# Strassen-like gate and up products: partial sums kept in one PSUM bank, with two alternating bank sets

## The reference, cut to what matters

```python
def channel_and_ple(h, p, g_ffn, w_gate, w_up, w_down, g_ple, w_ple_gate, w_ple_proj):
    n = rms_norm(h, g_ffn)
    h = h + (jax.nn.silu(n @ w_gate) * (n @ w_up)) @ w_down
    gate = jax.nn.sigmoid(rms_norm(h, g_ple) @ w_ple_gate)
    return h + gate * (p @ w_ple_proj)
```

## Time and profile before

| | |
|---|---|
| median of three runs | 2497.94 us (2497.43 to 2499.43) |
| span of the profiled execution | 2496.2 us |
| PE busy | 2467.4 us, 99% of the span, 20366 matmuls |
| DVE busy | 1755.7 us, 70% |
| ACT busy | 942.3 us, 38% |
| POOL busy | 255.1 us, 10% |
| granted clock of TensorE, mean | 0.996 of full speed |

### The profile page before, as it was taken

How to read it: one execution, slowest core, us unless ns; L and a number is a source line. 1 busy time by engine, 2 the same in 40 slices (tenths; PEclk the granted TensorE clock), 3 DMA queues, 4 the chain that set the end, 5 groups by cost and what they waited for, 6 DMA issues and landing times.

```text
span 2496.2 us, 51722 instructions
## 1 busy us (share of the span) xinstructions
PE 2467.4 (99%) x20366; PEld 2452.8 (98%) x20366; DVE 1755.7 (70%) x2206; ACT 942.3 (38%) x1226; POOL 255.1 (10%) x281
## 2 busy tenths in 40 slices
PE   7999999999999999999999999999999999999998
PEld 7999999999999999999999999999999999999998
DVE  5777787778787899888888888888433323456433
ACT  5344334333433454444444444444322221233331
POOL 1120111011110000000000000000000000143000
PEclk9999999999999999999999999999999999999999
DMA  6352333233343424333333334343665443233331
GB/s 210 120 159 93 129 109 127 98 121 110 119 149 99 150 93 162 122 132 135 118 135 118 135 120 146 122 150 110 223 220 165 161 146 117 80 90 108 108 114 68
DMA packets 99886, 324.02 MB, mean 130 GB/s; under 512 B 18274, under 2 KB 18786, under 8 KB 99312
## 3 DMA queue, kind: packets, MB, share of 16 engines
q1 hardware_dynamic: 72288, 250.25, 30.4%
q0 software_dynamic: 26672, 70.69, 8.1%
q10 hardware_dynamic: 864, 2.24, 0.2%
HBM read 286.80 MB, written 40.65 MB: 131 GB/s over the span
## 4 chain that ended last, share of the span: by engine, by line
PE 82%; DVE 9%; issue 3%; DMA 3%; ACT 1%; DVEq 0%; SPq 0%; ACTq 0%
PE acc L570 15%; PE acc L574 14%; PE acc L572 14%; PE acc L774 12%; PE acc L775 12%; PE acc L773 12%; DVE tmp L1525 2%; DVE wlo L1293 1%; DMA wraw<-in_w_down 1%; DMA skew<-skew_dram 1%; DVE tmp L1298 1%; ACT whi L929 1%; DVE q_both L1410 1%; DMA hid<-in_x_tiles 1%; PE aux L619 1%
## 5 line engine op out<-in xcount | busy, mean ns | idle before, releaser
L1293 DVE TENSOR_TENSOR wlo<-wraw,whi 128x1024 fp32r<-128x1024 f32 (+1 forms) x276 | 333.5, 1209 | 361.3 <-ACT whi L929 360.8
L929 ACT ACTIVATE whi<-wraw 128x1024 fp32r<-128x1024 f32 (+1 forms) x276 | 285.2, 1034 | 667.6 <-PE acc L574 593.1
L773 PE MATMUL acc<-xb_hi,whi 128*128 128x260 f32 x1228 | 347.9, 283 | 2.3 <-DVE xb_lo_t L1692 2.3
L774 PE MATMUL acc<-xa_lo,whi 128*128 128x260 f32 x1228 | 348.7, 284 | 0.0
L775 PE MATMUL acc<-xa_hi,wlo 128*128 128x260 f32 x1228 | 348.7, 284 | 0.0
L773 PE MATMUL acc<-xa_hi,whi 128*128 128x260 f32 x1228 | 347.3, 283 | 0.6 <-DVE wlo L1643 0.6
L775 PE MATMUL acc<-xb_hi,wlo 128*128 128x260 f32 x1228 | 347.5, 283 | 0.0
L570 PE MATMUL acc<-slots_a,whi 128*128 128x260 f32 x1536 | 312.8, 285 | 0.3 <-DVE wlo L1293 0.3
L574 PE MATMUL acc<-slots_a,wlo 128*128 128x260 f32 x1536 | 308.9, 282 | 0.0
L572 PE MATMUL acc<-slots_a,whi 128*128 128x260 f32 x1536 | 308.9, 283 | 0.0
L1104 ACT ACTIVATE whi<-wraw 128x1024 fp32r<-128x1024 f32 x176 | 186.4, 1059 | 223.0 <-PE acc L775 120.7
(11 more groups left out here) (309 smaller groups left out, 5111.4 us busy)
## 6 DMA issues: line engine op xcount, KB each, us to landing
wraw<-in_w_in SPq DMA_DIRECT2D x96, 512.0 KB, 3.6
blocks<-in_w_gate SPq DMA_DIRECT2D x88, 512.0 KB, 5.9
blocks<-in_w_up SPq DMA_DIRECT2D x88, 512.0 KB, 5.3
wraw<-in_w_down SPq DMA_DIRECT2D x48, 448.0 KB, 3.4
wraw<-in_w_out SPq DMA_DIRECT2D x32, 512.0 KB, 3.6
wraw<-in_w_ple_gate SPq DMA_DIRECT2D x32, 512.0 KB, 3.5
slots_b<-f_dram SPq DMA_DIRECT2D x28, 520.0 KB, 4.5
f_dram<-sig_t POOLq DMA_DIRECT2D x22, 520.0 KB, 3.2
```

What stands on the lines that cost most here:

```text
L773: mm(to, w_h, hi, start=p == 0, stop=False)
L774: mm(to, w_h, lo, start=False, stop=False)
L929: on(whi[:, u % HILO, 0:width], wraw[:, u % RAW, 0:width], ACT.Copy).then_inc(s_whi, 1)
L1293: V.tensor_tensor(wlo[:, u % HILO, 0:width], wraw[:, u % RAW, 0:width], whi[:, u % HILO, 0:width].bitcast(F32), ALU.subtract).then_inc(s_w ...
```

## The change

The operands' signs are turned so that products that are only added can be summed by PE in one bank. A pair's units write to three banks instead of four: units 0, 2, 4 and 6 to one bank (`z`), without starting it anew after unit 0; units 3 and 5 to a second (`x`); unit 1 to a third (`w`). Between them the partial sums are copied out: after unit 0 (`q0`), after unit 2 (`v2`), after unit 3 (`p5`) and after unit 6, all by ACT; DVE makes three combinations, after units 1, 4 and 5. PE waits for each copy before it adds to the bank again: unit 2 for `q0`, unit 4 for `v2`, unit 5 for `p5`, unit 6 for DVE's read after unit 4. Even and odd pairs use different banks. POOL's addition is gone.

The first pair keeps unit 2 in a bank of its own, and there DVE, not ACT, makes `v2` and `p5` from the product and `q0`.

With the order of the products the order of the weights' sums changes: sums 1 and 2 are made at `v` = 1 (before: 0), sums 3 and 4 at `v` = 3 after the low part (before: sum 3 at `v` = 2, sum 4 at `v` = 4). The multiplication by `rstd` (`pair_scaled`) moves from the end of a pair into the next one, and the steps on the result one unit or two further on. SyncE's queue waits for a single sum ahead of each block.

```diff
-X_OF = (0, 3, 1, 4, 5, 6, 2)
-Z_, X_, Y_, W_ = (0, 0), (0, 1), (1, 0), (1, 1)
-BANK_OF = (Z_, X_, Z_, Y_, W_, X_, Y_)
+X_OF = (0, 1, 3, 6, 4, 5, 2)
+STARTS = (0, 1, 3)
...
+    def banks_of(parity, first=False):
+        if first:
+            z, z1, w, x = bank((0, 0)), bank((0, 1)), aux[:, BANK_T, 0:HALF], bank((1, 0))
+        elif parity == 0:
+            z, z1, w, x = bank((0, 0)), bank((0, 0)), bank((1, 1)), bank((0, 1))
+        else:
+            z, z1, w, x = aux[:, BANK_T, 0:HALF], aux[:, BANK_T, 0:HALF], bank((1, 0)), aux[:, BANK_O, 0:HALF]
+        return z, w, z1, x, z1, x, z1
...
@@ PE, gate_up @@
                 if u == 2:
-                    pe.wait_ge(s_cp, it * 8 + (2 * r + 1))
-                if u == 3:
-                    pe.wait_ge(s_ev, it * 24 + 6 * r)
+                    pe.wait_ge(s_q0, n + 1)
+                if u == 3 and not (fresh and r < 2):
+                    pe.wait_ge(s_1a, n - 1)
+                if u == 4:
+                    pe.wait_ge(s_v2c, n + 1)
                 if u == 5:
-                    pe.wait_ge(s_ev, it * 24 + (6 * r + 1))
+                    pe.wait_ge(s_p5, n + 1)
                 if u == 6:
-                    pe.wait_ge(s_ev, it * 24 + (6 * r + 2))
-                triples(w, u, range(KP2)).then_inc(s_unit, 1)
+                    pe.wait_ge(s_1b, n + 1)
+                for p in range(KP2):
+                    done = triple(to[u], w, u, p, u in STARTS or first and u == 2)
+                done.then_inc(s_unit, 1)
...
@@ ACT, gate_up @@
+                    on(q0_t, to[0], ACT.Copy).then_inc(s_q0, 1)
+                if u == 2 and not first:
+                    act.wait_ge(s_1a, n)
+                    on(v2_t, to[2], ACT.Copy).then_inc(s_v2c, 1)
+                if u == 3 and not first:
+                    act.wait_ge(s_1b, n)
+                    on(p5_t, to[3], ACT.Copy).then_inc(s_p5, 1)
+                if u == 6 and not first:
+                    act.wait_ge(s_11, n + 1)
+                    on(tile[:, 0, HALF:T], to[6], ACT.Copy).then_inc(s_0b, 1)
...
@@ DVE, blocks_ahead @@
-            if v == 0:
+            if v == 1:
                 block_sum(at, it, r, 1)
                 block_sum(at, it, r, 2)
-            if v == 2:
+            block_lo(at, r, v)
+            if v == 3:
                 block_sum(at, it, r, 3)
-            if v == 4:
                 block_sum(at, it, r, 4)
-            block_lo(at, r, v)
...
@@ DVE, gate_up @@
+                if u == 0 and r % 2 == 0 and not first:
+                    pair_scaled(n - 1, up_t[:, :, :])
                 if u == 1:
+                    dve.wait_ge(s_q0, n + 1)
...
+                    V.tensor_tensor(tile[:, 0, 0:HALF], to[1], q0_t, ALU.add).then_inc(s_11, 1)
+                    if r % 2 == 1:
+                        pair_scaled(n - 1, gate_set)
+                    elif not first:
+                        hidden_last(it * 2 + r // 2 - 1, set_before)
+                if first and u == 2:
+                    V.tensor_tensor(v2_t, to[2], q0_t, ALU.add).then_inc(s_v2c, 1)
+                if first and u == 3:
+                    V.tensor_tensor(p5_t, to[3], q0_t, ALU.subtract).then_inc(s_p5, 1)
...
+                if u == 4:
+                    dve.wait_ge(s_p5, n + 1)
+                    V.tensor_tensor(tile[:, 1, HALF:T], p5_t, to[4], ALU.subtract).then_inc(s_1b, 1)
                 if u == 5:
+                    dve.wait_ge(s_v2c, n + 1)
+                    V.tensor_tensor(tile[:, 1, 0:HALF], to[5], v2_t, ALU.subtract).then_inc(s_1a, 1)
...
@@ GpSimd @@
-            G.tensor_tensor(tile, tile, q1_t, ALU.add).then_inc(s_c11, 1)
```

More of the change, by code:

```diff
@@ L772, in triple @@
             hi, lo = part_hi(p, n, n + 1).squeeze(1), part_lo(p, n, n + 1).squeeze(1)
[L773 to L781, removed]
+            mm(to, w_h, hi, start=begin and p == 0, stop=False, skip_group_check=not begin)
+            mm(to, w_h, lo, start=False, stop=False, skip_group_check=not begin)
+            return mm(to, w_l, hi, start=False, stop=p == KP2 - 1, skip_group_check=not begin)
         def first_products(at):
+            to = banks_of(0, True)
             for u in range(4):
                 pe.wait_ge(s_wlo, at.count(u))
-                if u in (0, 3):
-                    pe.wait_ge(s_read, T_D - 1 + u // 3)
-                if u == 2:
+                if u == 0:
+                    pe.wait_ge(s_read, T_D - 1)
+                if u == 1:
                     pe.wait_ge(s_pt2, 8 * KA)
+                if u == 3:
+                    pe.wait_ge(s_read, T_D)
                 for p in range(EARLY):
                     pe.wait_ge(s_xp, p + 1)
-                    triple(first_to(u), u, u, p)
+                    triple(to[u], u, u, p, True)
             for p in range(EARLY, KP2):
                 pe.wait_ge(s_lo_a, p - EARLY + 1)
-                done = triple(first_to(0), 0, 0, p)
+                done = triple(to[0], 0, 0, p, True)
             done.then_inc(s_unit, 1)
@@ L1165, in gate_up @@
             i = it * 2 + r // 2
+            n = it * TURN + r
             gate_set = tmp[:, r // 2 * 2:r // 2 * 2 + 2, :]
             first = fresh and r == 0
+            tile = gate_set if r % 2 == 0 else up_t[:, :, :]
+            to = banks_of(r % 2, first)
             for u in range(7):
                 w = 7 * r + u
-                act.wait_ge(s_unit, at.count(w))
+                if u in (0, 2, 3, 6) and not (first and u > 0):
+                    act.wait_ge(s_unit, at.count(w))
                 if u == 0:
                     if not first:
[L1173 to L1185, removed]
+                        act.wait_ge(s_11, n)
+                    if fresh and r == 1:
+                        act.wait_ge(s_0b, 1)
+                    on(q0_t, to[0], ACT.Copy).then_inc(s_q0, 1)
[8 more added lines that the diff above has]
+                    on(tile[:, 0, HALF:T], to[6], ACT.Copy).then_inc(s_0b, 1)
                 if first and u == 0:
@@ L1204, in gate_up @@
                     on(sig_t[:, :, :], gate_set, ACT.Sigmoid).then_inc(s_sig, 1)
-                if r % 2 == 0 and u == 1 and not first:
+                if r % 2 == 0 and u == 2 and not first:
                     hidden_hi(it * 2 + r // 2 - 1, tmp[:, (r // 2 + 1) % 2 * 2:(r // 2 + 1) % 2 * 2 + 2, :])
@@ L1760, in gate_up @@
             first = fresh and r == 0
+            to = banks_of(r % 2, first)
             for u in range(7):
                 w = 7 * r + u
-                if u in (1, 3, 5, 6):
+                if u in (1, 4, 5) or first and u in (2, 3, 6):
                     dve.wait_ge(s_unit, at.count(w))
+                if u == 0 and r % 2 == 0 and not first:
+                    pair_scaled(n - 1, up_t[:, :, :])
                 if u == 1:
[L1766 to L1769, removed]
@@ L1790, in gate_up @@
-                if r % 2 == 0 and u == 0 and not first:
-                    hidden_last(it * 2 + r // 2 - 1, set_before)
+                    dve.wait_ge(s_q0, n + 1)
+                    if r % 2 == 0 and not fresh:
+                        dve.wait_ge(d_flo[r // 2], it * 16)
+                    if r % 2 == 1:
+                        if fresh and r == 1:
+                            dve.wait_ge(d_h[3], 16)
+                        else:
+                            dve.wait_ge(s_f, i * 3 - 1)
@@ L1792, in gate_up @@
+                if first and u == 6:
+                    V.tensor_tensor(tile[:, 0, HALF:T], to[6], q0_t, ALU.add).then_inc(s_0b, 1)
+                    dve.wait_ge(s_nroot, N_FFN)
+                    V.reciprocal(rstd[:, :], rstd[:, :]).then_inc(s_ninv, 1)
+                    dve.wait_ge(s_ninv, N_FFN)
                 if first and u == 0:
@@ L2070, in load_residual @@
             pool.dma_start(res[:, m % 2, :], h_dram[:, m, :]).then_inc(l_res[m % 2], 16)
[L2072 to L2086 removed]
+        with pool.Fori(0, PAIRS // TURN) as it:
+            for half in range(2):
+                store_hidden(it * 2 + half, half)
         for g in range(4):
             pool.wait_ge(d_h[g], 16)
[L2090 removed]
         pool.wait_ge(d_flo[0], 16 * (PAIRS // 4))
```

160 lines of the change are left out of this document (79 added, 81 removed).

## The result

The changed kernel takes 2502.65 us (median of 12 runs, 2501.1 to 2504.61) against 2497.51 for the kernel before, run on the same chip: ratio 1.0022, 95% interval 1.0014 to 1.003. It is 5.1 us slower, as forecast (5.1; 2503.0). The profiled execution has a span of 2502.6 us.

The account below looks back on a forecast made before the run. PE was taken as the bound, busy 99% of the span. Stage 0, start 5.2 and end -0.1 gave 5.1 us on a span of 2496.2; with the median 1.7 above the span, 2503.0, range 2499.5 to 2510.

Parts of the forecast that it names:

- Inside the stage: Gate and up: PE stays busy, every copy is ready in time, and the change costs 0 us.
- The slack of 2.25 to 2.3 us: Gate and up: time to spare for copies (2.3 us) and DVE's read behind unit 4 (2.25 us) before PE waits.
- The rival of the late copy: DVE's read behind unit 4 comes 2.46 us late; PE waits 0.21 us in 43 pairs, 9 us: 2512; chance 14%.
- The start, the late halves: First pair: sums 3 and 4 stand ahead of the activations' late halves, which come 2.28 us later.
- `v2`'s place in DVE's order: First pair: `v2` stands behind unit 5's low part; PE can start unit 4 only at 897.60.
- Unit 4: First pair: unit 4 starts at 897.60 instead of 892.31, 5.3 us later.
- The clock: First pair: shift 5.3 us with unit 4 at 1.2 GHz, 2.8 at 2.4 GHz, 7.8 if low through unit 5; 5.2 taken.
- The case taken (unit 4 low again): First pair: unit 4 runs at 1.2 GHz as before, so the shift stays 5.3 us.
- The rival that the clock gives most of it back: First pair: the clock rises by PE's restart or early in unit 4; start costs 2.8 us, 2500.6; chance 18%.
- The end: Behind the last pair: low part releasing the next loads unmoved within 0.1 us, some loads earlier; -0.1 us taken.

Follow-up runs that it names:

- five multiplications: Changed kernel with five extra DVE multiplications, result thrown away, ahead of DVE's read behind unit 4 in 39 pairs: 2540.22 us, ratio 1.0176.
- both edits: Changed kernel; in the first pair sums 1 to 3 at their old places, `q0` and `v2` made right behind unit 4's low part: 2497.19 us, ratio 1.0005.
- the run in which the clock fell ahead of it: Against the kernel with both edits, DVE makes `p5` ahead of unit 6's low part in the first pair: 2497.35 us, ratio 1.0002.
- the three runs with spare work on DVE and ACT: Changed kernel with two or five extra DVE multiplications, or seven ACT copies, in 39 pairs: 2502.4, 2540.22 and 2564.2 us.
- spare matmuls that hold the clock: Changed kernel with 54 extra matmuls (9, 15, 30) filling PE's waits in the first pair, result thrown away: 2499.82 us, ratio 1.0011.
- seven copies: Changed kernel with seven extra ACT copies, result thrown away, ahead of the copy of `v2` in 39 pairs: 2564.2 us, ratio 1.0272.

## Why the prediction was right, step by step

- *Inside the stage, 0*: -0.28. No wait, 0.120 us a matmul, DVE at 84%. The slack of 2.25 to 2.3 us on which this rests measures 2.05 and 2.11, some 0.2 too generous, which cost nothing, since PE lists no wait there. The rival of the late copy is real past that point (five multiplications), and its price would have been higher: 2.46 us late is 0.41 us in 43 pairs, about 18 us and not 9. The -0.28 is the rest of the stage, 874.56 us in place of 874.84; no run shows what it comes from.
- *The start, the late halves*: +2.28 forecast, +2.27 measured. *`v2`'s place in DVE's order*: 4.95 us behind unit 4's low part, forecast and measured. *Unit 4*: +5.29 forecast, +5.39 measured, with a wait of 3.02 us. That this is the cause is shown by the runs that undo it: both edits bring unit 4's start, which unit 4's own clock can't change, from 21.18 to 16.39 (17.06 in the run in which the clock fell ahead of it), and unit 5 from 26.36 to 21.41.
- *The clock*: 5.2 us of shift forecast, 4.52 measured at unit 5. The case taken (unit 4 low again) came, but only in part: the clock rose during the wait, fell again, and rose within unit 4, which gave 0.87 us back. No run shows the 5.2 itself or that this case had to come, and the shift changes from execution to execution: the three runs with spare work on DVE and ACT have the same first pair, unit 4 starts at 21.17 in each, and unit 5 at 26.35, 26.34 and 26.99, a shift of 4.5 to 5.15 us from the kernel before. The rival that the clock gives most of it back did not come; with spare matmuls that hold the clock the time is 2499.82.
- *The end*: -0.1 forecast, +0.36 measured. The low part that releases the next loads comes 10.08 us behind down's first matmul (1789.32), before 10.07, so that reading was right. PE's wait for low weights, 0.96 us in place of 0.77, comes later, 24.67 us behind that matmul (before 24.31), and ends where a load of down's weights ends: it took 4.23 us from its issue to the start of its rounding, before 3.60. A wait of 0.28 us for a load of the hidden tile is new. Whether the change causes any of this is open: from down's first matmul to the end the twelve profiled executions take 722.6 to 723.8 us, so +0.36 lies within their scatter.

The sum of the profile without what lies ahead of the stage is 4.52 - 0.28 + 0.36 = 4.6 us, of the medians 5.1, of the forecast 5.1. The mechanism of the forecast is borne out, but that the number agrees to a tenth is luck: the clock's term was 0.7 too large, the end's 0.5 too small, and the executions scatter by more than that ahead of the stage.

The Trainium skill's rule on bursts behind waits (TensorE: Matmul & The Clock Gate, section "HAM oscillation — how this bites in real kernels"), weighed in the prediction, agrees with unit 4's first microseconds here (0.50 at 900 to 902). It does not hold each time: in the run with five multiplications unit 4 came behind a wait of 3.06 us, and the clock read 1.00 at 894 to 896, where it started, and 0.52 in the next 2 us.

## What to carry to other kernels

When products are accumulated in one bank with copies between, the steady state is safe as long as each copy has its slack, and that is a sum that can be made from the trace beforehand, to some 0.2 us here; what is lost is lost at the stage's ends, where a step that nobody waited for has become one that releases PE and still stands at its old place in the queue. Find each new release in its engine's order and put it ahead of all that PE doesn't wait for: here two moves of a few lines took the loss away, as far as the runs can tell. Where waits remain in a stretch with a fluctuating clock, judge a microsecond by many runs, and in the trace by distances from a common point.

## What the runs showed of the hardware that was not expected

- PE waited 0.76 us (five multiplications) and 1.37 us (seven copies) in each of 39 pairs, and the granted clock read 1.00 over the stage's window; in the first pair a single wait of 1.96 us was followed by 0.58 in one profiled execution, and one of 1.98 us by 1.00 in another. The Trainium skill (TensorE: Matmul & The Clock Gate, section "A second HAM failure mode: psum-queue depth-cycling") tells of a kernel in which frequent short idling between groups, as banks cycle, made the clock swing; in these two runs it did not.
- In the changed kernel's first pair the clock read 0.91 in a window with 0.50 us of matmul work, and 0.50 in the next, full of work.
- The stage's first matmul came between 873.1 and 879.9 us in twelve profiled executions whose programs hardly differ up to there, more than the change is worth.
